# Front attention: who multiplies the softmax probabilities by the reciprocal of their sum

## The chip, the cores and the metric

The kernel runs on one NeuronCore of one Trainium2 chip. The metric is the device time of one execution in microseconds (us). The five engines of the core run their own instruction streams and meet only at semaphores: PE (TensorE, matmuls; its weight loads are shown apart as PEld), DVE (VectorE), ACT (ScalarE), POOL (GpSimd) and SP (SyncE, which only issues DMAs here).

## The reference, cut to what matters

Two transformer blocks run one after the other on 256 tokens of width 2048, in float32. The first has two layers; each begins with one wide projection, out of which come a gated convolution and a banded attention of 16 heads. The part of the attention that the change touches is the softmax with a sink logit:

```python
u = rmsnorm(h) @ w_in                       # 44 blocks of 128 columns
s = einsum('bqkgd,bskd->bkgqs', qb, kb) * scale + bias_band
m = max(max(s, axis=-1), sink)
e = exp(s - m[..., None])
denom = sum(e, axis=-1) + exp(sink - m)
pr = (e / denom[..., None])                 # the scaling in question
out = einsum('bkgqs,bskd->bqkgd', pr, vb)   # 8 pairs of heads per layer
```

In the same stage a depthwise convolution of 31 taps runs over 8 blocks of 128 channels, and its LayerNorm needs the sum of all channels first (`y_sum` below).

## The kernel before, in words

All weights are cut into 350 units of 128 x 2048 numbers. To keep float32 accuracy in the faster fp32r format, each unit is split: ACT rounds it to `whi` (line 229), POOL or DVE computes the remainder `low` (lines 241 and 234), and PE multiplies both with an operand that is split too (lines 259, 260, 262). Four units are in flight; ACT rounds a unit two units ahead of the one that PE is on.

The stage in question is `phase_front`, run once in each of the two layers. It works through 46 units m = 0 to 45, and each engine has its order written out by hand as a Python loop over m, unrolled. After PE has finished unit m, ACT copies one half of the result out of PSUM (line 657), DVE adds the halves (line 692), scales (lines 699, 703), and ACT makes the tanh of a gate where the unit is one (line 563, function `gate`). Between these, DVE computes eight taps of the convolution per unit (lines 721, 723, 725, 736; the last sum is `y_sum`, line 738).

The attention goes by pairs of heads, h = 0 to 7, four units each, so a period of the stage is four units. For pair h: PE makes the scores after unit 9+4h (`scores`, line 868); DVE adds the bias and takes the maximum behind unit 10+4h (`biased`, lines 751, 755); ACT takes the exponential and its sum in unit 11+4h (`exps`, lines 572, 575), into the tile `sm`, one instruction for each of 4 rows of 257 numbers; DVE takes the reciprocal of the 4 sums and multiplies `sm` behind unit 11+4h (`normed`, lines 760, 761); PE transposes `sm` after unit 12+4h (`transposes`, line 876, 8 matmuls); ACT copies the result (`probs`, line 585) and PE multiplies it with the values after unit 13+4h (`values`, line 885).

Two single steps late in the stage matter as well. PE sums `y_sum` over the partitions inside unit 37 (`mean`, line 913), before that unit's fourth product. Then it sums the squares after units 38 and 39 (`variance`, line 892).

A wait on a semaphore holds an engine's whole queue: what stands behind it in the loop doesn't start. PE waits for `normed` before its first transpose.

Of the kernel before, what the change touches and what calls it, by code (L numbers as in the profile page):

```python
# [9 lines left out]
ALU = mybir.AluOpType  # L10
ACT = mybir.ActivationFunctionType
# [4 lines left out]
T = 256  # L16
# [129 lines left out]
def program(nc, xT, pT, weights, params, sinks, rel_bias, lora, positions, consts, onehot, band_mask, masks, inv_freq, table, chunk_mats, out):  # L146
    ctx = ExitStack()
    with ctx:
# [35 lines left out]
        st = place("st", [P, 3, 32])  # L184
# [27 lines left out]
        def spread(x, n, at=1):  # L212

            dims = [list(d) for d in x.ap]
            return bass.AP(tensor=x.tensor, offset=x.offset, ap=dims[:at] + [[0, n]] + dims[at:])
# [241 lines left out]
        for g in range(6):  # L457
# [3 lines left out]
        PAIRS = HEADS // 2  # L461
# [12 lines left out]
        sm = place("sm", [P, 4, T + 1], at=arena + 8960)  # L474
# [5 lines left out]
        fr_counts = {"p_in": 16, "p_hi": 1, "p_lo": 1, "gate": 24, "gated": 24, "y_first": 1, "sum_first": 1, "y_sum": 1,  # L480
                     "tok": 1, "v_read": 1, "k_read": 1,
                     "sink": 8, "scores": 8, "biased": 8, "top": 8, "neg": 8, "exps": 8, "probsT": 8, "probsT_read": 8,
                     "out": 8, "normed": 8, "mixed": 8, "hi": 8, "lo": 8,
                     "mean": 1, "centred": 1, "y_sq": 2, "var_mm": 2, "var": 1, "dev": 1, "inv": 1, "scaled": 1,
                     "affine": 8, "th": 8, "once": 8, "w": 8, "w_hi": 8, "w_lo": 8,
                     "e_even": 4, "e_odd": 2, "even_read": 3, "odd_read": 4}
# [15 lines left out]
        def phase_front(l, u0, op, nxt, ready=None, summed=None):  # L502
# [52 lines left out]
            def _(act):  # L555
# [13 lines left out]
                def exps(h):  # L569
# [7 lines left out]
                    if h + 1 < PAIRS:  # L577
                        act.wait_ge(*fr["exps"](h + 1))
                        put_sink(h + 1)

                def probs(h):
                    act.wait_ge(*fr["probsT"](h + 1))
                    if h:
                        act.wait_ge(*fr["out"](h))
                    act.activation(probsT[:, :, :], ps[:, 2:4, :], ACT.Copy).then_inc(fr["probsT_read"].sem, 1)
# [23 lines left out]
                def even(n):  # L609
                    act.wait_ge(*fr["e_even"](n // 2 + 1))  # L610
                    return act.activation(e_raw[:, 2 * n:2 * n + 2, :], ps[:, e_bank[n], :], ACT.Copy, scale=0.5)

                for m in range(46):
                    if m == 44:
                        even(0).then_inc(fr["even_read"].sem, 1)
                    if m >= 3 * ahead:
                        act_split(act, u0, m)
                    if m == 0:
                        if l == 0:
                            act_split(act, u0, 2)  # L620
                        stat_act(act, stat)
                    if m == 3:
                        act.wait_ge(*fr["p_in"](16))
                        act.activation(p_hl[:, :, 0:T], p_in[:, :, :], ACT.Copy).then_inc(fr["p_hi"].sem, 1)
                    if m == 7:
                        act.wait_ge(ev_done.sem, u0 + SLOTS.index(("k", 1)) + 3)
                        for x in range(2):
                            for e in range(2):
                                ins = act.activation(keysT[DH * e:DH * e + DH, x:x + 3:2, :], k_s[DH * x:DH * x + DH, :, :], ACT.Copy)
                        ins.then_inc(fr["k_read"].sem, 1)  # L630
                    if m == 8:
                        act.wait_ge(*fr["tok"](1))
                        act.activation(v_tok[:, :, :], ps[:, 2, :], ACT.Copy).then_inc(fr["v_read"].sem, 1)
                        put_sink(0)
                        act.wait_ge(*fr["y_first"](1))
                        act.activation(ps[:, 7, T:2 * T], y_ln[:, 0, :], ACT.Copy).then_inc(fr["sum_first"].sem, 1)
                    h, x = (m - 9) // 4, (m - 9) % 4
                    if x == 2 and 0 <= h < PAIRS:
                        exps(h)
                    if x == 0 and 1 <= h <= PAIRS:  # L640
                        probs(h - 1)
                    if x == 2 and 1 <= h <= PAIRS:
                        high(h - 1)
                    if m == 38:
                        act.wait_ge(*fr["centred"](1))
                        act.activation(y_sq[:, :, :], y_ln[:, 0:4, :], ACT.Square).then_inc(fr["y_sq"].sem, 1)
                    if m == 39:
                        act.wait_ge(*fr["var_mm"](1))
                        act.activation(y_sq[:, :, :], y_ln[:, 4:8, :], ACT.Square).then_inc(fr["y_sq"].sem, 1)
                    if 42 <= m:  # L650
                        conv_high(2 * (m - 42))
                        conv_high(2 * (m - 42) + 1)
                    if m < 36:
                        act.wait_ge(mm_done.sem, u0 + m + 1)
                        if m >= 2:
                            act.wait_ge(ev_done.sem, u0 + m + 1)
                        act.activation(halves[m % 2][:, 0:T], ps[:, bank_of(m), T:2 * T], ACT.Copy).then_inc(read.sem, 1)
                    if m in GATED:
                        gate(m)
                    if m == 40:  # L660
                        act.wait_ge(*fr["var"](1))
                        act.activation(t2[:, 0:T], t2[:, 0:T], ACT.Sqrt).then_inc(fr["dev"].sem, 1)
                    if m == 44:
                        even(2).then_inc(fr["even_read"].sem, 1)
                    if 41 <= m < 45:
                        affine(2 * (m - 41))
                        affine(2 * (m - 41) + 1)
                    if m == 44:
                        even(4).then_inc(ev_done.sem, 1)
                    if m == 45:  # L670
                        even(6).then_inc(fr["even_read"].sem, 1)
                        act.wait_ge(*fr["odd_read"](3))
                        act.activation(small[:, 5:6], small[:, 5:6], ACT.Copy).then_inc(ev_done.sem, 1)

            @stage.vector
            def _(v):
# [77 lines left out]
                    v.wait_ge(*fr["biased"](h + 1))  # L754
                    v.tensor_reduce(s[:, 0:4], sm[:, :, :], axis=AX.X, op=ALU.max).then_inc(fr["top"].sem, 1)

                def normed(h):
                    s = st[:, h % 3, :]
                    v.wait_ge(*fr["exps"](h + 1))
                    link(v.reciprocal(s[:, 24:28], s[:, 12:16]))  # L760
                    v.tensor_tensor(sm[:, :, 0:T], sm[:, :, 0:T], spread(s[:, 24:28], T, 2), ALU.mult).then_inc(fr["normed"].sem, 1)

                def mixed(h):
                    v.wait_ge(*fr["out"](h + 1))
# [28 lines left out]
                for m in range(44):  # L793
                    evict(m)
                    if m and m - 1 in GATED and SLOTS[m - 1][0] != "glu":
                        gated(m - 1)
                    h, x = (m - 10) // 4, (m - 10) % 4
                    if x == 0 and 0 <= h < PAIRS:
                        biased(h)
                    if x == 1 and 0 <= h < PAIRS:  # L800
                        normed(h)
                    if x == 0 and 1 <= h <= PAIRS:
                        mixed(h - 1)
                    if x == 2 and 1 <= h <= PAIRS:
                        low_part(h - 1)
                    if m == 6:
                        v.wait_ge(*fr["p_hi"](1))
                        v.tensor_tensor(p_hl[:, :, T:2 * T], p_in[:, :, :], p_hl[:, :, 0:T].bitcast(F32), ALU.subtract).then_inc(fr["p_lo"].sem, 1)
                    if 2 <= m < 6:
                        conv(m - 2, 0)  # L810
                    if 8 <= m < 36:
                        conv(m % 4, m // 4 - 1)
                    if SLOTS[m][0] == "glu":
                        gated(m)
                    if m == 37:
                        v.wait_ge(*fr["mean"](1))
                        v.scalar_tensor_tensor(y_ln[:, :, :], spread(ps[:, 5, 0:T], CB), -1.0 / (CB * P), y_ln[:, :, :], ALU.mult, ALU.add).then_inc(fr["centred"].sem, 1)
                    if m == 39:
                        v.wait_ge(*fr["var_mm"](2))
                        v.tensor_scalar(t2[:, 0:T], ps[:, 5, T:2 * T], 1.0 / (CB * P), EPS, ALU.mult, ALU.add).then_inc(fr["var"].sem, 1)  # L820
                    if m == 40:
                        v.wait_ge(*fr["dev"](1))
                        v.reciprocal(ps[:, 5, 0:T], t2[:, 0:T]).then_inc(fr["inv"].sem, 1)
                        v.wait_ge(*fr["inv"](1))
                        v.tensor_tensor(y_ln[:, :, :], y_ln[:, :, :], spread(ps[:, 5, 0:T], CB), ALU.mult).then_inc(fr["scaled"].sem, 1)
                    if m >= 42:
                        conv_low(2 * (m - 42))
                        conv_low(2 * (m - 42) + 1)
                    if m >= 41:
                        product(2 * (m - 41))  # L830
                        product(2 * (m - 41) + 1)
# [1630 lines left out]
```

## Time and profile before

| | us |
|---|---|
| median of 3 runs (lowest, highest) | 2212.02 (2211.22, 2212.11) |
| the profiled execution, device time | 2211.91 |
| its span, first to last instruction | 2210.1 |
| PE busy | 2171.5 (98%) |
| DVE busy | 1713.3 (78%) |
| ACT busy | 1071.8 (48%) |
| POOL busy | 544.9 (25%) |

The two front stages lie at about 26 to 309 us and 499 to 783 us of the span. Busy shares are averages over stages with different limits, so a stage's own rows have to be read. A row of the timeline has its start, its length, engine, line, what is written and read, and how many equal instructions it stands for; in square brackets is the time for which the engine was idle before it and what ended this. Consecutive instructions of an engine overlap a little, so the distance between two starts is what one costs its queue, and is shorter than its length.

### The profile page before, as it was taken

The page shows a single profiled execution, that of the slowest core. Times are in us where ns is not written, and L with a number is a line of the kernel's source. Part 1 is how long each engine was busy: PE and PEld are TensorE (multiplying, and loading weights), DVE is VectorE, ACT ScalarE, POOL GpSimd, SP SyncE. Part 2 cuts the span into 40 slices and gives each one's busy share as a digit, 9 for nine tenths or more (in the row PEclk, how much of TensorE's full clock was granted, in tenths as well). Part 3 has the DMA queues.
Part 4 walks back from the last instruction along what each step waited for, and adds up shares of the span by engine and source line. Part 5 has one row for each costly group of instructions (what it writes and reads, how often), then busy time and mean ns, then how long its engine had stood idle before and what let it go on. Part 6 is the DMA issues. An engine that isn't in the chain of part 4 may idle for free.

```text
span 2210.1 us, 38356 instructions
## 1 busy us (share of the span) xinstructions
PE 2171.5 (98%) x14358; PEld 1895.5 (86%) x14358; DVE 1713.3 (78%) x2889; ACT 1071.8 (48%) x1435; POOL 544.9 (25%) x225
## 2 busy tenths in 40 slices
PE   7999999999999999999999999999999999999997
PEld 6888888888888788899999887888888888888886
DVE  7799778886899588888888666888888884447887
ACT  5555464445555554556555534444444443333454
POOL 4776731018776620210003312100000000000001
PEclk9999999999999999999999999999999999999999
DMA  7555445555555455554455300555555555555564
GB/s 253 187 175 180 160 172 187 187 181 207 177 179 183 142 183 191 186 191 171 154 170 182 93 22 19 210 182 183 188 189 190 190 187 184 183 188 189 190 211 170
DMA packets 69030, 384.73 MB, mean 174 GB/s; under 512 B 15088, under 2 KB 22768, under 8 KB 23984
## 3 DMA queue, kind: packets, MB, share of 16 engines
q1 hardware_dynamic: 68912, 383.09, 48.8%
q8 instruction: 82, 1.34, 0.3%
q14 instruction: 36, 0.29, 0.0%
HBM read 379.89 MB, written 3.18 MB: 173 GB/s over the span
## 4 chain that ended last, share of the span: by engine, by line
PE 70%; POOL 14%; issue 11%; DVE 2%; ACT 1%; DMA 1%; SPq 0%; POOLq 0%; DVEq 0%; ACTq 0%
PE ps L259 33%; PE ps L260 18%; POOL low L241 14%; PE ps L247 4%; PE ps L248 3%; PE ps L249 3%; PE ps L262 2%; DMA raw<-weights_dram 1%; PE ps L1858 1%; PE ps L1910 0%; PE ps L1902 0%; PE ps L1710 0%; PE ps L1847 0%; PE ps L298 0%; PE ps L1919 0%
## 5 line engine op out<-in xcount | busy, mean ns | idle before, releaser
L259 PE MATMUL ps<-opA,whi 128*128 128x512 f32 x2460 | 872.6, 395 | 0.0
L260 PE MATMUL ps<-opA,low 128*128 128x256 f32 x2624 | 707.4, 280 | 0.2 <-DVE opA L980 0.2
L229 ACT ACTIVATE whi<-raw 128x2048 fp32r<-128x2048 f32 x346 | 660.3, 1909 | 79.7 <-DMA raw<-weights_dram 78.3
L234 DVE TENSOR_TENSOR low<-raw,whi 128x2048 fp32r<-128x2048 f32 x252 | 583.7, 2317 | 67.3 <-ACT whi L229 51.5
L259 PEld LDWEIGHTS ps<-opA,whi 128*128 128x128 f32 x2460 | 461.8, 188 | 106.3 <-issue 3.0
L241 POOL TENSOR_TENSOR low<-raw,whi 128x2048 fp32r<-128x2048 f32 x95 | 436.3, 4608 | 412.2 <-ACT whi L229 385.8
L259 PE MATMUL ps<-opB,whi 128*128 128x512 f32 x1380 | 494.2, 398 | 15.0 <-DVE opB L418 12.6
L260 PEld LDWEIGHTS ps<-opA,low 128*128 128x128 f32 x2624 | 492.7, 188 | 14.6 <-DVE opA L980 0.5
L260 PE MATMUL ps<-opB,low 128*128 128x256 f32 x1472 | 397.5, 280 | 0.0
L259 PEld LDWEIGHTS ps<-opB,whi 128*128 128x128 f32 x1380 | 260.0, 188 | 78.2 <-DVE low L412 10.4
L268 ACT ACTIVATE crossed<-ps 128x256 f32<-128x256 f32 x168 | 64.4, 383 | 492.4 <-PE ps L262 492.2
L260 PEld LDWEIGHTS ps<-opB,low 128*128 128x128 f32 x1472 | 277.6, 189 | 7.6
L723 DVE SCALAR_TENSOR_TENSOR ps<-a_in,par,ps 128x256 f32<-128x256 f32 x464 | 226.8, 489 | 14.6
L259 PE MATMUL ps<-act_hl,whi 128*128 128x512 f32 x672 | 237.3, 394 | 0.1
L1123 POOL MEMSET ssq<- 128x256 f32 (+1 forms) x4 | 1.5, 366 | 805.0 <-DVE t L972 677.1
L260 PE MATMUL ps<-act_hl,low 128*128 128x256 f32 x704 | 191.5, 279 | 0.0
L247 PE MATMUL ps<-opB,whi 128*128 128x256 f32 x560 | 161.2, 288 | 0.2 <-DVE ps L1432 0.2
L249 PE MATMUL ps<-opB,low 128*128 128x256 f32 x560 | 158.1, 282 | 0.0
L248 PE MATMUL ps<-opB,whi 128*128 128x256 f32 x560 | 157.8, 282 | 0.0
L259 PEld LDWEIGHTS ps<-act_hl,whi 128*128 128x128 f32 x672 | 126.0, 187 | 30.8 <-issue 2.0
L260 PEld LDWEIGHTS ps<-act_hl,low 128*128 128x128 f32 x704 | 132.0, 187 | 2.6
L1127 POOL TENSOR_TENSOR ssq<-ssq,sq 128x256 f32<-128x256 f32 (+1 forms) x63 | 60.6, 963 | 249.2 <-ACT sq L1040 184.3
(393 smaller groups left out, 2608.0 us busy)
## 6 DMA issues: line engine op xcount, KB each, us to landing
raw<-weights_dram SPq DMA_DIRECT2D x350, 1024.0 KB, 4.8
bias_t<-table_dram SPq DMA_DIRECT2D x16, 384.0 KB, 5.9
hT<-xT_dram SPq DMA_DIRECT2D x4, 512.0 KB, 8.9
out_dram<-hT SPq DMA_DIRECT2D x3, 512.0 KB, 2.8
lora_g<-lora_dram SPq DMA_DIRECT2D x1, 1024.0 KB, 5.0
p_in<-pT_dram SPq DMA_DIRECT2D x2, 256.0 KB, 5.1
lora_wa<-lora_dram SPq DMA_DIRECT2D x1, 512.0 KB, 5.6
chunk_mats_dram<-compact SPq DMA_DIRECT2D x4, 128.0 KB, 3.1
```

Source lines behind the costliest of these rows:

```text
L229: act.activation(whi[:, v % RING, :], raw[:, v % RING, :], ACT.Copy).then_inc(hi_done.sem, 1)
L234: v_.tensor_tensor(wlo(v % RING, 0, width), raw[:, v % RING, 0:width], whi[:, v % RING, 0:width].bitcast(F32), ALU.subtract).then_inc(lo_d ...
L241: pool.tensor_tensor(wlo(v % RING), raw[:, v % RING, :], whi[:, v % RING, :].bitcast(F32), ALU.subtract).then_inc(lo_done.sem, 1)
L247: pe.matmul(dst, whi[:, s, w0:w0 + P], op[:, k, 0:T], start=start, stop=False)
L248: pe.matmul(dst, whi[:, s, w0:w0 + P], op[:, k, T:2 * T], start=False, stop=False)
L249: return pe.matmul(dst, wlo(s, w0, w0 + P), op[:, k, 0:T], start=False, stop=stop)
L259: pe.matmul(*cross, start=start, stop=False)
L260: mm = pe.matmul(ps[:, b, 0:T], wlo(s, w0, w0 + P), op[:, k, 0:T], start=False, stop=False)
L262: mm = pe.matmul(*cross, start=False, stop=True)
L268: act.activation(crossed[:, b, :], ps[:, b if bank is None else bank, T:2 * T], ACT.Copy).then_inc(read.sem, 1)
L723: link(v.scalar_tensor_tensor(y, taps, w, y, ALU.mult, ALU.add))
L1127: pool.tensor_tensor(total, total, part, ALU.add).then_inc(summed.sem, 1)
```

## The change

DVE no longer multiplies. Its step `over` takes only the reciprocal of the 4 sums and signals it. ACT gets the step `normed`: four activations with function Copy, one for each row of 128 x 256 numbers, each with one number per partition as its scale (a pointer to the reciprocal). ACT makes them at the head of its loop turn m = 12+4h, ahead of the rounding of weight unit m+2; DVE's `over` stays where `normed` was, behind unit 11+4h. PE's wait for `normed` is the same, but ACT signals it now.

```diff
+                def normed(h):
+                    s = st[:, h % 3, :]
+                    act.wait_ge(*fr["over"](h + 1))
+                    for x in range(4):
+                        ins = act.activation(sm[:, x, 0:T], sm[:, x, 0:T], ACT.Copy, scale=s[:, 24 + x:25 + x])
+                    ins.then_inc(fr["normed"].sem, 1)
...
                 for m in range(46):
                     if m == 44:
                         even(0).then_inc(fr["even_read"].sem, 1)
+                    if m % 4 == 0 and 12 <= m < 12 + 4 * PAIRS:
+                        normed(m // 4 - 3)
                     if m >= 3 * ahead:
                         act_split(act, u0, m)
...
-                def normed(h):
+                def over(h):
                     s = st[:, h % 3, :]
                     v.wait_ge(*fr["exps"](h + 1))
-                    link(v.reciprocal(s[:, 24:28], s[:, 12:16]))
-                    v.tensor_tensor(sm[:, :, 0:T], sm[:, :, 0:T], spread(s[:, 24:28], T, 2), ALU.mult).then_inc(fr["normed"].sem, 1)
+                    v.reciprocal(s[:, 24:28], s[:, 12:16]).then_inc(fr["over"].sem, 1)
...
                     if x == 1 and 0 <= h < PAIRS:
-                        normed(h)
+                        over(h)
```

ACT's program around m = 12 before (t_62 is the gate's input, whi the rounded weights, probsT the transposed probabilities, t_63 and t_64 the halves copied out of PSUM):

```order
45 L563 ACTIVATE ps<-t_62 128x256
46 L229 ACTIVATE whi<-raw 128x2048
47 L657 ACTIVATE t_63<-ps 128x256
48 L229 ACTIVATE whi<-raw 128x2048
49 L585 ACTIVATE probsT_92<-ps 128x1024
```

The same place now (lines are numbered anew behind the inserted code; line 585 is the new scaling, 592 and 666 are the old 585 and 657):

```order
45 L563 ACTIVATE ps<-t_62 128x256
46 L585 ACTIVATE sm<-sm,st 128x256 x4
47 L229 ACTIVATE whi<-raw 128x2048
48 L666 ACTIVATE t_63<-ps 128x256
49 L229 ACTIVATE whi<-raw 128x2048
50 L592 ACTIVATE probsT_92<-ps 128x1024
```

Four activations stand between the gate's tanh and the rounding of the next weight unit; nothing else moves on ACT.

DVE's program behind unit 11+4h before (y_ln is the finished convolution of a block of channels):

```order
77 L692 TENSOR_TENSOR ps<-ps,t_64 128x256
78 L703 TENSOR_TENSOR t_62<-ps,rs 128x256
79 L760 RECIPROCAL st<-st 128x4
80 L761 TENSOR_TENSOR sm<-sm,st 128x4x256
81 L723 SCALAR_TENSOR_TENSOR ps<-a_in,par,ps 128x256 x6
82 L725 SCALAR_TENSOR_TENSOR y_ln<-a_in,par,ps 128x256
```

And now:

```order
76 L701 TENSOR_TENSOR ps<-ps,t_64 128x256
77 L712 TENSOR_TENSOR t_62<-ps,rs 128x256
78 L769 RECIPROCAL st<-st 128x4
79 L732 SCALAR_TENSOR_TENSOR ps<-a_in,par,ps 128x256 x6
80 L734 SCALAR_TENSOR_TENSOR y_ln<-a_in,par,ps 128x256
```

The multiplication is gone, and the convolution's taps follow the reciprocal at once.

## Rows read from the trace of the kernel before

**Rows 1.** The page: busy time of PE, and the chain that ended last.

```profile
PE 2171.5 (98%) x14358; PEld 1895.5 (86%) x14358; DVE 1713.3 (78%) x2889; ACT 1071.8 (48%) x1435; POOL 544.9 (25%) x225
...
PE 70%; POOL 14%; issue 11%; DVE 2%; ACT 1%; DMA 1%; SPq 0%; POOLq 0%; DVEq 0%; ACTq 0%
```

**Rows 2.** Busy time in one period: length, PE, PEld, DVE, ACT, POOL, clock, DMA.

```profile
118.50:144.10 25.60, 25.60 (x155) 21.62 (x154) 23.89 (x50) 13.06 (x24) 18.37 (x5) 1.00 0.53 180
```

**Rows 3.** Timeline, DVE, layer 0, pair 1.

```profile
107.06 0.43 DVE L692 TENSOR_TENSOR ps<-ps,t 128x256 f32<-128x256 f32 x1 [1.05 <-ACT t L657]
...
115.64 0.42 DVE L703 TENSOR_TENSOR t<-ps,rs 128x256 f32<-128x256 f32 x1
115.98 0.17 DVE L760 RECIPROCAL st<-st 128x4 f32<-128x4 f32 x1
116.19 1.23 DVE L761 TENSOR_TENSOR sm<-sm,st 128x1024 f32<-128x1024 f32 x1
117.33 3.11 DVE L723 SCALAR_TENSOR_TENSOR ps<-a_in,par,ps 128x256 f32<-128x256 f32 x6
```

**Rows 4.** Timeline, PEld and PE, the transposes of pair 1.

```profile
117.47 0.94 PEld L876 LDWEIGHTS ps<-ident,sm 128*128 128x128 f32 x8
...
117.61 1.04 PE L876 MATMUL ps<-ident,sm 128*128 128x128 f32 x8
```

**Rows 5.** Timeline, ACT, around turn m = 12+4h of pair 1.

```profile
116.10 0.39 ACT L563 ACTIVATE ps<-t 128x256 f32<-128x256 f32 x1 [2.22 <-DVE t L703]
116.42 1.90 ACT L229 ACTIVATE whi<-raw 128x2048 fp32r<-128x2048 f32 x1
...
120.30 1.01 ACT L585 ACTIVATE probsT<-ps 128x1024 f32<-128x1024 f32 x1
```

**Rows 6.** Line 384: timeline of 8, and shortest/median/longest ns of one.

```profile
8.41 3.31 ACT L384 ACTIVATE opB<-hT,par 128x256 fp32r<-128x256 f32 x8 [0.86 <-DMA hT<-xT_dram]
...
L384 ACT ACTIVATE opB<-hT,par x16: 492/492/507, 8.4 to 17.0; 128x256 fp32r<-128x256 f32 x16
```

**Rows 7.** Timeline, PE, the same 8 matmuls without and with a wait.

```profile
262.35 1.89 PE L892 MATMUL ps<-y_sq,ones 128*128 128x256 f32 x8
...
270.12 1.99 PE L892 MATMUL ps<-y_sq,ones 128*128 128x256 f32 x8 [0.26 <-ACT y_sq L649]
```

**Rows 8.** Timeline, ACT and PE, pair 0 of layer 0.

```profile
90.19 0.39 ACT L563 ACTIVATE ps<-t 128x256 f32<-128x256 f32 x1 [2.16 <-DVE t L703]
...
92.02 1.03 PE L876 MATMUL ps<-ident,sm 128*128 128x128 f32 x8
```

**Rows 9.** Timeline, DVE and PE, the sum of the channels in layer 0.

```profile
248.90 0.42 DVE L738 TENSOR_TENSOR y_sum<-ps,y_ln 128x256 f32<-128x256 f32 x1
...
247.34 0.28 PE L260 MATMUL ps<-opB,low 128*128 128x256 f32 x1
249.38 0.70 PE L913 MATMUL ps<-y_sum,ones 128*128 128x256 f32 x2 [1.76 <-DVE y_sum L738]
```

**Rows 10.** Timeline, PE, behind that sum in layers 0 and 1; a stretch's clock.

```profile
254.56 1.08 PE L885 MATMUL ps<-probsT,v_tok 128*64 128x256 f32 x8
...
722.06 0.70 PE L913 MATMUL ps<-y_sum,ones 128*128 128x256 f32 x2 [1.77 <-DVE y_sum L738]
...
728.80 1.08 PE L885 MATMUL ps<-probsT,v_tok 128*64 128x256 f32 x8
...
723.30:726.50 3.20, 3.20 (x13) 2.71 (x12) 0.44 (x2) 3.00 (x3) 0.98 (x2) 0.52 0.00 0
```

**Rows 11.** Timeline, POOL and PE: remainders of two units; the first one's products.

```profile
118.40 9.14 POOL L241 TENSOR_TENSOR low<-raw,whi 128x2048 fp32r<-128x2048 f32 x2 [4.93 <-ACT whi L229]
...
126.27 0.50 PE L259 MATMUL ps<-opB,whi 128*128 128x512 f32 x1
```

**Rows 12.** Timeline, PE and ACT, pair 7 of layer 0.

```profile
277.57 1.03 PE L876 MATMUL ps<-ident,sm 128*128 128x128 f32 x8
...
279.35 0.39 ACT L563 ACTIVATE ps<-az 128x256 f32<-128x256 f32 x1 [5.65 <-DVE az L711]
```

More of the change, by code:

```diff
@@ L482, in program @@
                      "sink": 8, "scores": 8, "biased": 8, "top": 8, "neg": 8, "exps": 8, "probsT": 8, "probsT_read": 8,
-                     "out": 8, "normed": 8, "mixed": 8, "hi": 8, "lo": 8,
+                     "out": 8, "over": 8, "normed": 8, "mixed": 8, "hi": 8, "lo": 8,
                      "mean": 1, "centred": 1, "y_sq": 2, "var_mm": 2, "var": 1, "dev": 1, "inv": 1, "scaled": 1,
```

## The prediction

> **What bounds the kernel now.** I read the page's busy line and the chain that ended last first: PE is busy for 98% of the span, and the chain is mostly PE [rows 1]. The chain's POOL share is work that runs in parallel with PE, so the next view is the busy time by stretches, laid over one period of the front stage (four weight units, one pair of heads). There PE is busy for all of 25.60 us, DVE for 23.89, ACT for 13.06 and POOL for 18.37, at the full granted clock [rows 2]. The reader is to see two things: PE sets the pace, so relief of DVE alone is worth nothing in an ordinary period; and DVE is nearly full, so where PE does wait for DVE it will be here. Then I went to the timelines, engine by engine, around the transposes, which wait for the step that is moved, and looked for every place in the stage where PE has idle time in brackets. There are two of some size per layer: before the sum over the channels (1.76 us in layer 0, 1.77 in layer 1 [rows 9, 10]), which waits for DVE, and a small one before the second sum of squares (0.26 us [rows 7]), which waits for ACT's exponentials and isn't touched.
>
> **What is removed.** DVE loses one multiplication of 128 x 1024 per pair, 8 in each of 2 layers. It starts at 116.19 and the next instruction at 117.33, so each costs DVE's queue 1.14 us [rows 3], 18.2 us in all. In an ordinary period that is worth nothing: DVE starts each period by waiting (1.05 us in this one) for what PE has just finished [rows 3], so what it gains becomes a longer wait there.
>
> **What is added, and whether it is in time.** ACT gets four activations per pair, with 256 numbers per partition and a pointer as scale. The trace has just this form in line 384: one lasts 492 ns, and 8 take 3.31 us, so a further one costs (3.31 - 0.49) / 7 = 0.40 us [rows 6]. Four take 0.49 + 3 x 0.40 = 1.70 us. They start when the gate's tanh lets go of ACT. DVE's reciprocal ends at 116.15 [rows 3], before the tanh ends, so the new wait for it is met. The instruction behind the tanh starts at 116.42 [rows 5]; with the scaling there, `sm` is ready at 116.42 + 1.70 = 118.12. Before, DVE had it ready at 116.19 + 1.23 = 117.42, and PE's weight load for the transposes started at 117.47, 0.05 us later, with the matmuls at 117.61 [rows 3, 4]. That matmul start was set by PE's own stream: the same distance stands where the wait was met long before. So the old step was just in time, and the new one is not: the weight load starts at 118.12 + 0.05 = 118.17 and the first matmul is recorded at about 118.18, 0.57 us late. A waiting group also restarts less tightly: the same 8 matmuls take 1.89 us without and 1.99 with a wait [rows 7], 0.10 more. I take 0.67 us per pair.
>
> On that 0.10 the Trainium skill, "TensorE: Matmul & The Clock Gate", section "Architectural detail: the array is 16× 32×32, not 1× 128×128", says that a matmul can begin before its weights are fully loaded. By that rule the restart would cost nothing and the sum would be 12 x 0.10 = 1.2 us lower; the pair of rows speaks against it, and I go by the rows.
>
> This is a delay relative to PE, and it repeats. What leads to the tanh hangs on PE: the tanh waits for DVE's line 703, which ends a run of DVE work that began with a wait for PE's unit 10+4h [rows 3, 5]. A later PE makes all of this as much later, so the delay doesn't heal in the next period. By pairs:
> - Pair 0: the tanh starts at 90.19, so the scaling at 90.51, its end at 92.21, the matmul at 92.27 in place of 92.02 [rows 8]: 0.25 + 0.10 = 0.35 us.
> - Pairs 1 to 5: 0.67 each, 3.35 us (the other periods have the distances of pair 1).
> - Pair 6: its delay falls into the wait for `y_sum`, next part.
> - Pair 7: the transposes are at 277.57, and ACT, which has done its scaling some 4 us earlier, then waits 5.65 us for DVE [rows 12]. Nothing.
>
> Bounds for one pair: nothing, if the scaling ran in the pipeline's shadow; above, four activations end to end, 4 x 0.49 = 1.97 us, 0.27 more than I take.
>
> **Where DVE's relief pays.** `y_sum` ends at 248.90 + 0.42 = 249.32, and PE starts its sum at 249.38; PE's last matmul before it starts at 247.34 [rows 9]. DVE's run up to `y_sum` is without gaps from the multiplication of pair 6 on, so it is ready 1.14 us earlier, at 248.18, and PE can start at 248.24. PE comes there at about 247.34 + 0.11 (256 columns at 2.4 GHz) + 0.67 = 248.12, delayed by pair 6, so it still waits a little and the whole 1.14 us is gained, with the delay of pair 6 inside the old wait. 1.14 us in each layer.
>
> **The clock.** In layer 1 the wait before `y_sum` is followed by a stretch of 3.2 us with a granted clock of 0.52, the 1.2 GHz level [rows 10]. From the sum to the values of pair 6 it takes 254.56 - 249.38 = 5.18 us in layer 0 and 728.80 - 722.06 = 6.74 us in layer 1 [rows 9, 10], for the same work: the low clock costs 1.56 us. With a wait of about 0.1 us in place of 1.8, I expect it not to fall, as it doesn't behind the small waits in the stage. So 1.56 us are gained. The Trainium skill's same page, section "HAM oscillation — how this bites in real kernels", has the rule that longer idle gaps of TensorE bring the half clock back. Layer 1 agrees; layer 0, with the same gap and no fall, shows that the gap alone doesn't decide it, which is why the clock has a rival of its own.
>
> **What is queued behind the new work.** ACT's rounding of the next two weight units moves 1.70 us later, and with it POOL's remainders. The first of these takes 9.14 / 2 = 4.57 us from 118.40, so it ends at 122.97, and PE wants it at 126.27 [rows 11]: a margin of 3.3 us, of which 1.70 is used, while PE comes 0.67 later. The copy of the transposed probabilities moves from 120.30 to 122.00 [rows 5] and ends at 123.0; PE needs it for the values, which, with the next pair's scores, last about 1 us each [rows 10] and stand before 126.27, so at about 124. No weight load by DMA hangs on ACT's step, since a slot comes free by PE's end of a unit. I cost all of these at nothing; if the cover were gone, each us of lateness would be a us of PE, up to 14 times.
>
> **The sum.** Per layer 0.35 + 3.35 - 1.14 = 2.56; two layers 5.12; less the clock, 5.12 - 1.56 = 3.56 us. The profiled execution took 2211.91 us (span 2210.1), 0.11 below the median of 2212.02. So 2215.5 us. A change within 0.2%, 4.4 us, can't be told from none; its upper edge is 2216.4.
>
> **Rivals.**
> - *The clock isn't given back* (slower): it still falls to 1.2 GHz once, in layer 1 or behind one of the new waits of 0.67 us, of which there are ten. For it: the fall in layer 1 and not in layer 0 behind equal gaps. Against it: the gap shrinks to a tenth. One such stretch costs 1.56 us: 2217.1, 0.23% above the median. It decides as soon as one stretch of 3.2 us shows a clock near 0.5.
> - *The activations don't overlap*: 1.97 us for four. Twelve waits grow by 0.27, and pair 6 reaches past `y_sum` by about 0.2 in each layer: 3.6 us more, 2219.1. Against it: line 384's eight do overlap.
> - *The scaling is shorter*: the tanh, of the same size without a pointer, lets ACT go after 116.42 - 116.10 = 0.32 us [rows 5]. Four would take 0.39 + 3 x 0.32 = 1.35 us, the wait shrinks to 0.32, and pair 0 has none: 10 x 0.32 - 2.28 - 1.56 = -0.6, 2211.3. If no wait at all came, -3.84: 2208.1, not even then 0.2% faster.
> - *The rounding comes too late*: POOL's remainder misses PE. It needs the scaling to cost more than 3.3 us; with 1 us short per pair it would be 14 us more, 2229.
>
> **How the numbers follow.** Forecast 0.66, clock 0.14, no overlap 0.08, shorter 0.09, rounding 0.03. The forecast's own range is 2213.9 to 2217.0 (the 0.10 of the restart off, or 0.10 more per wait); about 0.10 of its 0.66 lie above 2216.4. Slower: 0.14 + 0.08 + 0.03 + 0.10 = 0.35. Faster: 0.03, a part of the shorter case with something unseen on top. The rest, 0.62, is no change. The range takes in the clock's case and reaches nearly to the shorter one: 2211.8 to 2218.3.
>
> **What would show it.** The scaling: length of four near 1.70 us, starting at the end of the tanh. PE's transposes of pairs 1 to 5 with an idle of about 0.5 to 0.7 us before them, released by ACT's scaling. The period from one pair's transposes to the next 0.67 longer than before. PE's idle before line 913's successor near zero, and no granted clock of 0.5 in layer 1's front. POOL's remainders later and PE never waiting for them. The prediction is wrong if the transposes show no idle, if the period stays at 25.6, or if the clock falls somewhere new.

## The result and the profile after

| | before | changed |
|---|---|---|
| median of 20 runs each (lowest, highest), us | 2211.46 (2208.86, 2213.58) | 2214.27 (2213.29, 2216.03) |
| ratio of the changed kernel to before, 95% interval | | 1.0016 (1.0009, 1.0022) |
| the profiled execution, us | 2211.91 | 2214.44 |
| its span, us | 2210.1 | 2212.7 |

The ratio says 3.5 us slower (2.0 to 4.9). The difference of the medians is 2.8 us, that of the two profiled executions 2.5. In these two traces the front stages alone make 2.65 us of difference, 2.13 in layer 0 and 0.52 in layer 1 (table below).

The page of the changed kernel first, its busy line:

```profile
PE 2172.4 (98%) x14358; PEld 1893.4 (86%) x14358; DVE 1689.2 (76%) x2873; ACT 1098.0 (50%) x1499; POOL 547.3 (25%) x225
```

DVE is busy for 24.1 us less, ACT for 26.2 more, and PE's work is the same [rows 1]. None of it says whether the kernel got slower. The timelines do. ACT and PE around turn m = 12+4h of pair 1, layer 0:

```profile
116.44 0.39 ACT L563 ACTIVATE ps<-t 128x256 f32<-128x256 f32 x1 [2.22 <-DVE t L712]
116.76 1.69 ACT L585 ACTIVATE sm<-sm,st 128x256 f32<-128x256 f32 x4
118.36 1.90 ACT L229 ACTIVATE whi<-raw 128x2048 fp32r<-128x2048 f32 x1
...
122.23 1.01 ACT L592 ACTIVATE probsT<-ps 128x1024 f32<-128x1024 f32 x1
```

```profile
117.71 0.40 PE L262 MATMUL ps<-opB,whi 128*128 128x512 f32 x1
118.50 1.09 PE L884 MATMUL ps<-ident,sm 128*128 128x128 f32 x8 [0.40 <-ACT sm L585]
119.35 0.48 PE L259 MATMUL ps<-opB,whi 128*128 128x512 f32 x1
...
144.71 1.09 PE L884 MATMUL ps<-ident,sm 128*128 128x128 f32 x8 [0.41 <-ACT sm L585]
```

The four activations take 1.69 us, end at 118.45, and the transposes start 0.05 later. The bracket's 0.40 understates the loss, since the modelled end of the last matmul hangs over; the distance from pair to pair tells it: 144.71 - 118.50 = 26.21 us, where it was 143.20 - 117.61 = 25.59. So 0.62 us per pair. The sum over the waits in the changed kernel's trace shows the same group (engine, line, what was waited for, total us, times, longest):

```profile
PE ps L884 <- ACT sm L585: 4.8, 12, 0.4
```

The same for the weight loads:

```profile
PEld ps L884 <- ACT sm L585: 9.5, 14, 0.7
...
PEld ps L921 <- DVE y_sum L747: 0.4, 2, 0.2
```

There are 12 long waits at the transposes, and the wait for the sum over the channels, 1.76 us in [rows 9] and 1.77 in [rows 10], is down to 0.2 on the weight load's side. The same place of the changed kernel in layer 0, PE, then DVE:

```profile
251.53 0.70 PE L921 MATMUL ps<-y_sum,ones 128*128 128x256 f32 x2
```

```profile
251.06 0.42 DVE L747 TENSOR_TENSOR y_sum<-ps,y_ln 128x256 f32<-128x256 f32 x1
```

And DVE behind unit 11+4h, against [rows 3]:

```profile
115.98 0.42 DVE L712 TENSOR_TENSOR t<-ps,rs 128x256 f32<-128x256 f32 x1
116.32 0.17 DVE L769 RECIPROCAL st<-st 128x4 f32<-128x4 f32 x1
116.40 3.08 DVE L732 SCALAR_TENSOR_TENSOR ps<-a_in,par,ps 128x256 f32<-128x256 f32 x6
```

From the reciprocal to the next tap it was 1.35 us and is 0.08: DVE is relieved of 1.27 us per pair, not 1.14, since its own wait behind the reciprocal has gone too. The granted clock of the changed kernel is full in layer 1, both from pair 6's transposes to past the sum and behind it, where it had fallen before [rows 10]. Two rows in the columns of [rows 2]:

```profile
724.30:727.90 3.60, 3.60 (x23) 3.13 (x23) 3.46 (x8) 1.90 (x2) 1.78 (x1) 1.00 0.83 282
727.50:730.70 3.20, 3.20 (x20) 2.80 (x19) 0.48 (x2) 2.96 (x3) 3.20 (x2) 1.00 0.17 67
```

POOL and the rounding behind the scaling: POOL's remainders start at 120.33 in place of 118.40, and PE's unit 14 at 127.22 with no wait.

```profile
120.33 9.17 POOL L241 TENSOR_TENSOR low<-raw,whi 128x2048 fp32r<-128x2048 f32 x2 [6.52 <-ACT whi L229]
```

```profile
127.22 0.49 PE L259 MATMUL ps<-opB,whi 128*128 128x512 f32 x1
```

### The profile page after: what moved, and what is told of

The parts are those of the page before. It is cut to its first block, busy times and chain, and to the rows that moved or that the text cites. A ratio compares the mean times of both kernels' runs of the same rounds, so it can differ in the third digit from the quotient of the medians.

```text
span 2212.7 us, 38404 instructions
## 1 busy us (share of the span) xinstructions
PE 2172.4 (98%) x14358; PEld 1893.4 (86%) x14358; DVE 1689.2 (76%) x2873; ACT 1098.0 (50%) x1499; POOL 547.3 (25%) x225
## 4 chain that ended last, share of the span: by engine, by line
PE 68%; issue 14%; POOL 12%; DVE 3%; ACT 1%; DMA 1%; SPq 0%; POOLq 0%; DVEq 0%; ACTq 0%
PE ps L259 32%; PE ps L260 17%; POOL low L241 12%; PE ps L247 4%; PE ps L249 3%; PE ps L248 3%; PE ps L262 2%; DMA raw<-weights_dram 1%; PE ps L1866 1%; PE ps L1918 0%; PE ps L1910 0%; PE ps L1718 0%; PE ps L1855 0%; POOL ssq L1135 0%; PE ps L298 0%
## 5 line engine op out<-in xcount | busy, mean ns | idle before, releaser
L260 PEld LDWEIGHTS ps<-opA,low 128*128 128x128 f32 x2624 | 491.9, 187 | 14.6 <-DVE opA L988 0.5
L732 DVE SCALAR_TENSOR_TENSOR ps<-a_in,par,ps 128x256 f32<-128x256 f32 x464 | 226.5, 488 | 14.6
```

The costliest lines, as they stand in the source:

```text
L260: mm = pe.matmul(ps[:, b, 0:T], wlo(s, w0, w0 + P), op[:, k, 0:T], start=False, stop=False)
L732: link(v.scalar_tensor_tensor(y, taps, w, y, ALU.mult, ALU.add))
```

## The experiments

The yardstick is read on PE in each trace: from pair 0's scores in a layer to the first of the small matmuls that end the stage (74.03 to 297.17 before, layer 0). It leaves out the program's start, where the clock can be low too. "Clock" is the mean over all runs of the granted clock of the whole run; one stretch like that of [rows 10] takes 0.0007 off it. "Us against before" goes by the ratio and its interval. "Clock fell" marks a stage with a stretch at the 1.2 GHz level, as in [rows 10]. The diffs below are cut to the lines that matter.

| kernel | layer 0, us | layer 1, us | clock (runs) | us against before |
|---|---|---|---|---|
| before | 223.14 | 224.72 (clock fell) | 0.9970 (77) | |
| the change | 225.27 | 225.24 | 0.9976 (20) | +3.5 (2.0, 4.9) |
| e1, ACT scales pair 6 only | 221.91 | 221.96 | 0.9976 (11) | -3.1 (-5.1, -1.1) |
| e2, ACT scales pairs 0 to 5 | 228.14 (clock fell) | 226.58 | 0.9967 (7) | +6.4 (4.0, 9.1) |
| e3, half the rows each | 222.65 | 222.64 | 0.9976 (11) | -2.2 (-4.2, -0.2) |
| e4, the scaling earlier | 221.90 | 221.91 | 0.9978 (11) | -3.8 (-5.7, -1.8) |
| e5, before with a later sum | 222.59 | 222.59 | 0.9976 (11) | -3.1 (-5.1, -1.1) |
| e6, the change with a later sum | 225.13 | 225.15 | 0.9976 (11) | +2.4 (0.4, 4.6) |
| e7, no pointer | 223.14 | 223.12 | 0.9972 (11) | -0.9 (-2.9, 1.1) |
| e8, e4 with a later sum | 221.33 | 221.36 | 0.9973 (11) | -4.4 (-6.4, -2.4) |
| f1, before, gap filled | 223.17 | 223.17 | 0.9973 (11) | -0.7 (-2.7, 1.3) |
| f2, rounding before scaling | 240.79 (clock fell twice) | 240.82 (clock fell twice) | 0.9943 (4) | +36.7 (33.2, 40.0) |

**e1, ACT scales only where its lateness is hidden.** In the changed kernel, both engines' steps ask for the pair:

```diff
 # DVE, in over(h)
+if not (h == 6):
+    v.wait_ge(*fr["over"](h + 1))
+    v.tensor_tensor(sm[:, :, 0:T], sm[:, :, 0:T], spread(s[:, 24:28], T, 2), ALU.mult).then_inc(fr["normed"].sem, 1)
 # ACT, in normed(h)
+if not (h == 6):
+    return
```

> ACT scales only in pair 6 of each layer; DVE multiplies in the other seven. Theory (the transposes wait for ACT's scaling in pairs 0 to 5, and DVE's relief is collected only at the sum over the channels): no new wait in pairs 0 to 5, period 25.6 us, pair 6's wait hidden in the old one, the sum over the channels 1.1 to 1.3 us earlier in each layer; 2.2 to 2.6 us faster than before, plus up to 1.56 us where the clock fell before. Rival (the cost of the change comes from the weight rounding behind the scaling on ACT, which is late for POOL): gain too, but with PE waiting for a remainder in unit 38. Rival (DVE's relief adds up over the pairs): little gain, under 0.5 us.

The stage takes 1.2 us less than before in layer 0. In layer 1 it takes 2.76 less, which is 1.2 and the clock's 1.56. The transposes of pairs 0 to 5 are at the old distance and only pair 6's wait (0.40 in the bracket); PE never waits in unit 38. DVE's relief in one pair gives all that its relief in eight gave: the earlier ones are swallowed by the period. Both rivals fall.

**e2, the complement.** The same with `h < 6` in place of `h == 6`.

> ACT scales only in pairs 0 to 5; DVE multiplies in pairs 6 and 7. Theory: the new waits stay (0.3 us in pair 0, 0.62 in each of pairs 1 to 5, 3.4 per layer, 6.8 in all), and the wait before the sum over the channels is back at 1.7 to 1.8 us: 6.8 us slower than before, and 3 to 4 us slower than the change as it was. Rival (DVE's relief adds up over the pairs): the wait before the sum stays near 0.1 and the time that of the change, 2.8 us above before.

Layer 1 takes 226.58, that is 3.4 us above the undisturbed 223.14, as expected, and the wait before the sum is back. Here the clock fell in layer 0 and not in layer 1. PE of e2, and a stretch of it:

```profile
252.96 0.90 PE L926 MATMUL ps<-y_sum,ones 128*128 128x256 f32 x2 [1.78 <-DVE y_sum L749]
```

```profile
253.90:257.10 3.20, 3.20 (x12) 2.68 (x12) 0.74 (x3) 2.70 (x3) 0.95 (x2) 0.55 0.00 0
```

**e3, half the rows for each engine.** PE waits for both parts.

```diff
 # ACT
-for x in range(4):
+for x in range(2, 4):
 # DVE, behind the reciprocal
+v.tensor_tensor(sm[:, 0:2, 0:T], sm[:, 0:2, 0:T], spread(s[:, 24:26], T, 2), ALU.mult).then_inc(fr["normed"].sem, 1)
```

> The scaling is shared in each pair: ACT scales rows 2 and 3, DVE rows 0 and 1. Theory: ACT's two take 0.49 + 0.40 = 0.89 us, ready at 116.76 + 0.89 = 117.65 in the terms of the changed kernel, ahead of PE's own arrival (117.8), so no wait at the transposes and a period of 25.6; DVE is relieved of half, some 0.6 us, collected at the sum over the channels: 1.2 us faster than before, plus the clock where it fell. Rival (any ACT work there delays PE through the rounding behind it): period still above 25.6, by about half of 0.62. If DVE and ACT hinder each other on the same tile, both parts are longer than 0.6 and 0.89.

ACT's two take 0.90 us and DVE's 0.69. No wait at the transposes, 25.59 us from pair to pair. The sum's wait is 1.23, so 0.5 us gained per layer. For 0.45 us both work on the same tile, and nothing of it shows in ACT's time; for DVE's 0.69 there is no row of it alone to compare with. ACT and DVE of e3:

```profile
115.41 0.90 ACT L585 ACTIVATE sm<-sm,st 128x256 f32<-128x256 f32 x2
```

```profile
115.17 0.69 DVE L771 TENSOR_TENSOR sm<-sm,st 128x512 f32<-128x512 f32 x1
```

**e4, the same work earlier.** All of the scaling stays on ACT.

```diff
 # DVE, unit m = 11+4h
+over((m - 11) // 4)
 evict(m)
-over(h)
 # ACT, turn m = 11+4h in place of the head of turn 12+4h
+normed((m - 11) // 4)
 gate(m)
```

> All of the scaling on ACT as in the change, but earlier: DVE takes the reciprocal ahead of unit 11+4h's halves, and ACT scales ahead of that unit's tanh. Theory: ACT was idle there for 2.2 us, so the scaling is ready near PE's arrival or before it, no wait at the transposes, period 25.6, tanh 1.1 to 1.7 us later at no cost, the sum over the channels 1.1 to 1.4 us earlier per layer: 2.2 to 2.8 us faster than before (plus the clock), 5 to 7 us faster than the change. Rival (the rounding, just as late as in the change, is what costs): stays at the change's time, 2.8 us above before.

ACT of e4, then PE, then PE at the sum over the channels:

```profile
115.72 1.71 ACT L585 ACTIVATE sm<-sm,st 128x256 f32<-128x256 f32 x4 [1.51 <-DVE st L769]
117.34 0.37 ACT L563 ACTIVATE ps<-t 128x256 f32<-128x256 f32 x1
117.65 1.90 ACT L229 ACTIVATE whi<-raw 128x2048 fp32r<-128x2048 f32 x1
```

```profile
117.71 0.40 PE L262 MATMUL ps<-opB,whi 128*128 128x512 f32 x1
117.95 1.04 PE L884 MATMUL ps<-ident,sm 128*128 128x128 f32 x8
...
248.47 0.70 PE L921 MATMUL ps<-y_sum,ones 128*128 128x256 f32 x2 [0.49 <-DVE y_sum L747]
```

The four activations now stand where ACT was idle for 2.2 us. They end at 117.43, ahead of PE; the transposes wait for nothing, and the rounding starts 0.9 us later than before the change, reckoned from PE's transposes, at no cost. This is the change with its gain and without its price: 1.24 us per layer below the undisturbed 223.14, and faster than before by the interval.

**e5 and e6, the sum later in PE's program.** In the kernel before (e5) and the changed one (e6):

```diff
-within=(3, mean) if m == 37
+within=(9, mean) if m == 37
```

> The kernel before with one number changed: PE sums the channels before the tenth product of unit 37 in place of the fourth, six products (2.1 us) later. Theory: the wait of 1.8 us before that sum is gone in both layers with no relief of DVE at all, about 1.9 us each, and with the gap the stretch at the 1.2 GHz level behind it (1.56 us where there is one): 3.8 us faster, up to 5.4. Rival (the clock falls for another reason): 3.8 us and a stretch near 0.5 in the front stages still.

> The changed kernel with the same one number changed. Theory: DVE's relief has nothing left to pay there, since the wait is gone anyway, and pair 6's wait of 0.62 us at the transposes is no longer hidden: 0.5 us slower to 0.3 faster than the change, that is 2.5 to 3.3 us above the kernel before, and 6.5 to 8 us above the kernel before with the later sum. Rival (relief of DVE pays elsewhere too): clearly faster than the change, by 2 us or more.

e5 missed: 0.55 us per layer, not 1.9. The time over the runs, 3.1 us below before, would have hidden this: it has the clock's gain in it and is near the 3.8 expected. The wait before the sum is gone, but PE waits 1.39 us for the next thing instead, the copied probabilities of pair 6. DVE, ACT and PE of e5:

```profile
249.24 0.42 DVE L738 TENSOR_TENSOR y_sum<-ps,y_ln 128x256 f32<-128x256 f32 x1
249.58 0.69 DVE L272 TENSOR_REDUCE ps<-ps 128x256 f32<-128x512 f32 x1
250.30 0.42 DVE L703 TENSOR_TENSOR az<-ps,rs 128x256 f32<-128x256 f32 x1
250.64 0.41 DVE L711 SCALAR_TENSOR_TENSOR bz_s<-ps,bz_s 128x256 f32<-128x256 f32 x1
```

```profile
251.15 0.39 ACT L563 ACTIVATE ps<-az 128x256 f32<-128x256 f32 x1 [4.57 <-DVE bz_s L711]
251.47 1.90 ACT L229 ACTIVATE whi<-raw 128x2048 fp32r<-128x2048 f32 x1
253.28 1.00 ACT L585 ACTIVATE probsT<-ps 128x1024 f32<-128x1024 f32 x1
```

```profile
254.33 1.08 PE L885 MATMUL ps<-probsT,v_tok 128*64 128x256 f32 x8 [1.39 <-ACT probsT L585]
```

Read backwards: PE waits for ACT's copy, which stands behind a rounding and a tanh, and the tanh waits for DVE's results, which come straight behind `y_sum`. The same late DVE holds PE twice, some 5 us apart, and the first wait hid the second. So DVE's relief has a second taker there, which I had missed. e6 is as fast as the change (225.13 against 225.27 in layer 0), as expected against before within its interval, but only 2.5 us per layer above e5 and not 3.3 to 4, because e5 kept that wait.

**e8, both.** e4 with the later sum.

> The early scaling on ACT together with the later sum over the channels. Theory: neither wait is left in pairs 0 to 6; as fast as the kernel before with the later sum alone (3.8 to 5.4 us below before), not faster, since DVE's relief has no taker left. Rival (relief of DVE pays at the end of the stage): 1 us or more faster than that.

DVE, then PE's weight load for the values, of e8:

```profile
248.00 0.42 DVE L747 TENSOR_TENSOR y_sum<-ps,y_ln 128x256 f32<-128x256 f32 x1
253.10 0.63 PEld L893 LDWEIGHTS ps<-probsT,v_tok 128*64 128x64 f32 x8 [0.45 <-ACT probsT L592]
```

In the yardstick e8 is 1.25 us per layer faster than e5. `y_sum` is 1.24 us earlier than in e5 and the values 1.23: this is DVE's relief once more, now collected at the second wait. "Not faster than e5" was wrong for the reason just found. The times over all runs can't show it: the medians differ by 1.0 us and the intervals overlap. In the yardstick e8 is 0.56 us per layer faster than e4; over all runs their intervals overlap, so which is the best isn't settled. Both beat the kernel before and the changed one: medians 2208.21 and 2207.93.

**e7, what the pointer costs.**

```diff
-ACT.Copy, scale=s[:, 24 + x:25 + x]
+ACT.Copy, scale=0.5
```

> The changed kernel with a constant 0.5 as scale of ACT's four activations in place of the pointer to the reciprocals: the probabilities aren't normalised, so this leaves out the division by the sum. It measures what the pointer costs. Theory: a further activation costs 0.32 us in place of 0.40 and the last one lasts 0.39 in place of 0.49, so four take 1.35 in place of 1.69, the wait per pair falls from 0.62 to about 0.28 us and pair 0 has none: 10 x 0.34 + 0.6 = 4 us faster than the change, about 1 us faster than before. Rival (the wait is that for the semaphore between the engines, not the length): period unchanged at 26.2.

The ACT row of e7:

```profile
116.69 1.32 ACT L585 ACTIVATE sm<-sm 128x256 f32<-128x256 f32 x4
```

Four take 1.32 us, 0.37 less than with the pointer; the period is 25.83 us, 0.38 less than 26.21. One for one: PE's wait is the length of ACT's work. 2.1 us per layer less than the change, as expected. (The probabilities aren't divided by their sum here.)

**f1, the gap without the idleness.** 16 matmuls of 256 columns in `mean`, ahead of the wait:

```diff
 def mean():
+    for _ in range(16):
+        pe.matmul(ps[:, 4, 0:T], whi[:, (u0 + 37) % RING, 0:P], op[:, 0, 0:T], start=True, stop=True)
```

> The kernel before with 16 matmuls of 256 columns into an unused piece of PSUM, 1.7 us, put into PE's wait for the sum over the channels in each layer; the wait stays as long for everything else. Theory (the gap of 1.8 us is what lets the clock fall in one of the layers): from pair 0's scores to the stage's end 223.1 us in both layers, as before without a fall; no granted clock near 0.5 in the front stages, mean clock over the runs 0.9976 as in the kernels without the gap, not 0.9970; 0.5 to 1.5 us faster than before though PE does more. Rival (the fall has nothing to do with the gap): stretch near 0.5 in one layer still, mean clock 0.9970, time that of before or up to 0.3 us above.

The stage takes 223.17 us in both layers, with no fall in either. But in this trace the clock fell elsewhere, in the second block, a row of f1:

```profile
1250.00:1258.00 8.00, 6.45 (x45) 5.93 (x44) 3.82 (x14) 3.23 (x11) 0.00 (x0) 0.79 0.01 3
```

The filling isn't needed for that one: e7 and e8 have such a fall at the same place without it. In all twelve traces PE waits 1.55 us there for DVE, and in these three the clock fell behind it. The mean clock of f1, 0.9973, lies midway between the two that were expected, and the time can't tell either. Half a confirmation.

**f2, a later scaling and an earlier rounding.** In turn 12+4h of the changed kernel:

```diff
-normed(m // 4 - 3)
 act_split(act, u0, m)
+normed(m // 4 - 3)
```

> The changed kernel with ACT's two steps at the head of turn 12+4h swapped: the weight unit is rounded first, as early as before the change, and the probabilities are scaled behind it. Theory (PE waits for the scaling at the transposes): the wait grows by the 1.81 us that the rounding takes ACT's queue, to 2.4 us in pairs 1 to 5 and 2.1 in pair 0, and pair 6 is late past the sum over the channels by 1.7: some 12.5 us per layer, 25 us slower than the change, 28 above before; a clock that falls behind the new gaps adds to it. Rival (the change costs time because the rounding is late for POOL): back to the time of the kernel before or below it.

ACT and PE of f2, and a stretch of it:

```profile
118.90 1.90 ACT L229 ACTIVATE whi<-raw 128x2048 fp32r<-128x2048 f32 x1
120.70 1.69 ACT L585 ACTIVATE sm<-sm,st 128x256 f32<-128x256 f32 x4
```

```profile
122.44 1.09 PE L884 MATMUL ps<-ident,sm 128*128 128x128 f32 x8 [2.20 <-ACT sm L585]
```

```profile
122.30:129.30 7.00, 6.86 (x33) 6.08 (x34) 5.80 (x13) 3.07 (x4) 7.00 (x2) 0.76 0.53 184
```

The rival that blamed the late rounding is dead: with the rounding early the kernel is 37 us slower. The undisturbed distance between pairs is 28.00 us (122.44 to 94.44), 1.80 more than in the change. Two distances of layer 0 are 29.5, each with a clock that fell behind a gap of 2.2 us, and two of layer 1's gaps have such a fall as well, some 1.55 us each. Without them the stage takes 14.6 us more than 223.14 in each layer, 29.1 in both, where 28 were foreseen. Four falls add 6.2, and the trace of before has one fall of its own, 1.6: that makes 33.7, and the two profiled executions differ by 33.8 (2245.67 and 2211.91). The three other runs of f2 took 1.9 to 2.7 us longer than its profiled one, at a mean clock of 0.994 in place of 0.995; more falls in them are likely, but they have no trace.

## Why the prediction was right

The forecast was 2215.5, 3.5 us above the median shown then; measured were 2214.27 and a ratio worth 3.5 us. The mechanism came as forecast. That the two 3.5 agree to a tenth is luck: the interval is 2.0 to 4.9, the medians differ by 2.8, and two terms of the sum were too large, as follows. By steps:

- **Four activations take 1.70 us, and the scaling is 0.57 us late at the transposes.** 1.69 us, and the lateness follows ACT's length one for one (e7: 0.37 us shorter, period 0.38 shorter; f2: 1.81 later, period 1.80 longer). Shown.
- **0.10 us more for the restart.** Too much. The same transposes take 1.09 us behind a wait and 1.04 without [rows 4], so 0.05, and 0.62 per pair in place of 0.67. That is between the rows I went by and the rule of the Trainium skill's "TensorE: Matmul & The Clock Gate", section "Architectural detail: the array is 16× 32×32, not 1× 128×128", by which it would be nothing.
- **Pair 0 pays 0.35, pair 7 nothing.** 0.29 (from its scores to the next pair's 25.88 us in place of 25.59), and no wait in pair 7. Right.
- **DVE's relief is worth nothing in an ordinary period and 1.14 us at the sum over the channels.** The first half is shown by e1. The size was 1.27, since the wait behind DVE's reciprocal, which the change removes with the multiplication, costs its queue too: 0.29 + 5 x 0.62 - 1.27 = 2.12 us per layer, measured 2.13 in layer 0, where I had 2.56. What the prediction didn't see is that PE was held by the same late DVE once more at pair 6's values (e5). It made no difference here, because the change makes DVE itself earlier, and with it both waits shorter.
- **1.56 us for the clock.** Of the traces, the two with a gap of 1.76 to 1.78 us before the sum show one fall each, in layer 1 (before) and in layer 0 (e2), and f2 shows four, each directly behind a gap of 2.2 us. The nine others, whose longest gap in the stage is 1.39 us, show none in either front stage. That agrees with the rule that the prediction took from the Trainium skill's "TensorE: Matmul & The Clock Gate", section "HAM oscillation — how this bites in real kernels". Over the runs the clock rose from 0.9970 to 0.9976, worth 1.3 us rather than 1.56. That figure is rough: the kernels without the gap lie between 0.9972 (e7) and 0.9978 (e4), and falls also come at the program's start and in the second block in some executions and not in others. That the idleness causes the fall is likely and not settled: f1 is only half a confirmation, but the program's start, in the last section, speaks for it too.
- **Nothing behind the scaling on ACT is late.** POOL's remainders came 1.9 us later, 1.0 of it relative to PE's transposes, and PE didn't wait. f2, with the rounding early and 37 us lost, rules out that the late rounding is what costs.

The sum: 2 x 2.12 less 1.3 is 2.9 us, inside the interval of 2.0 to 4.9. The two errors in size, 0.4 us per layer too much for the stage and 0.3 us too much for the clock, partly cancelled.

## What to carry to other kernels

Before work goes from a full engine to an idle one, look at what waits for its result: here the old step ended 0.05 us before it was wanted, so each tenth that the new one took longer was lost in each pair, while the relief paid in one place per layer. An idle engine has its slack at particular times; the same work, put 1 us earlier into ACT's own wait, turned 3 us of loss into 3 to 4 us of gain (2.5 of it in the two stages, the rest the clock). And a wait that ends late can hide a second one with the same cause a few us on: removing the first by a later place in the program gave 0.55 us, not 1.9.

## What the runs showed of the hardware that was not expected

- The low clock moves. In executions of one and the same kernel before, the mean granted clock ranged from 0.995 to 0.998 and the time with it, over 77 runs: 2215.0 us at 0.995 (2 runs), 2213.4 at 0.996 (15), 2211.6 at 0.997 (42), 2210.0 at 0.998 (18). Three quarters of the variance of these times goes with the clock as it is listed, to three decimals.
- It can fall behind one gap of PE and not behind an equal one: 14 gaps of 1.9 to 2.2 us in f2, four falls; twelve equal gaps of 1.55 us in the second block, one in each trace, three falls.
- At the program's start the length of one gap differs by itself from execution to execution, for the same instructions. PE waits at about 17 us for DVE's operand, between 1.22 and 2.31 us. In the nine traces in which this gap was 1.66 us or more, the clock fell at its end, for some 3 us; in the three in which it was 1.22, 1.24 and 1.56 us (f1, e3, e1) it didn't. That is what speaks most for the idleness as the cause; the gap and what comes before it are not those of the front stage, so the lengths aren't to be carried over. PE at the gap and the clock behind it (0.51 and 1.00), before and then e1:

```profile
17.04 0.79 PE L259 MATMUL ps<-opB,whi 128*128 128x512 f32 x1 [2.18 <-DVE opB L418]
17.20:20.40 3.20, 3.20 (x11) 2.71 (x12) 3.11 (x8) 2.76 (x3) 0.00 (x0) 0.51 1.07 344
```

```profile
17.41 0.50 PE L259 MATMUL ps<-opB,whi 128*128 128x512 f32 x1 [1.56 <-DVE opB L418]
17.20:20.40 3.20, 2.99 (x15) 2.31 (x16) 3.13 (x9) 2.78 (x4) 0.00 (x0) 1.00 1.02 322
```

- ACT took no longer while DVE worked on the same tile: 0.90 us for two rows, against 0.49 + 0.40 worked out from [rows 6]. For DVE's part no run shows its time alone.
